# The norms of the second block beside its last products, on one Trainium2 core

## The reference

```
x = layer_norm(ALPHA * x + gate * out, g, b)        # out: mixer or mlp, gate: one row of 1024 per stream
z = x * (1 + scale) + shift                          # the next product's input
```

## Time and profile before

| What | Value |
|---|---|
| time, median of 3 runs | 2361.1 us (2357.43 to 2363.76) |
| the profiled execution's own time | 2361.36 us |
| its span | 2359.6 us |
| TensorE matmul busy | 2093.7 us (89%) |
| VectorE busy | 1306.8 us (55%) |
| ScalarE busy | 866.1 us (37%) |
| GpSimd busy | 229.3 us (10%) |
| mean granted clock of TensorE | 0.937 |

### The profile page before, as it was taken

The page is one execution under the profiler, slowest core; times in us unless marked ns, Lnnn a source line. Parts: engine busy times, 40 slices in busy tenths (PEclk is TensorE's granted clock), DMA queues, the critical chain, the costliest instruction groups (busy, mean ns, idle before and its releaser), DMA issues.

```text
span 2359.6 us, 31254 instructions
## 1 busy us (share of the span) xinstructions
PE 2093.7 (89%) x12126; PEld 1734.4 (74%) x12126; DVE 1306.8 (55%) x2032; ACT 866.1 (37%) x1435; POOL 229.3 (10%) x233
## 2 busy tenths in 40 slices
PE   6978899979788999599999993999999398996995
PEld 5856699878567998477777773888888387775985
DVE  4464677574646774454544448444444724756665
ACT  4422266344222663323223223322322323643442
POOL 1010200000101000000000004000000520612002
PEclk8999899989998999799999995999999699997998
DMA  7466556544664655222122231233323143433661
GB/s 204 135 230 203 168 166 181 188 125 135 226 215 138 178 178 196 83 72 89 53 89 71 71 89 36 90 92 93 100 89 104 35 111 108 60 77 110 191 188 54
DMA packets 304172, 296.26 MB, mean 126 GB/s; under 512 B 10390, under 2 KB 223586, under 8 KB 303952
## 3 DMA queue, kind: packets, MB, share of 16 engines
q1 hardware_dynamic: 297184, 276.86, 38.5%
q0 software_dynamic: 6896, 18.13, 3.6%
HBM read 293.90 MB, written 1.05 MB: 125 GB/s over the span
## 4 chain that ended last, share of the span: by engine, by line
PE 79%; DVE 14%; ACT 3%; issue 2%; DMA 1%; POOL 1%; SPq 0%; DVEq 0%; ACTq 0%; POOLq 0%
PE ps L422 22%; PE ps L423 22%; PE ps L424 22%; DVE w_lo L411 2%; PE ps L2048 2%; PE ps L1689 2%; PE ps L488 2%; DVE small L1367 1%; DVE zt_lo L1522 1%; PE ps L665 1%; PE ps L2038 1%; DVE hid L1422 1%; PE ps L663 1%; PE ps L1537 1%; DVE y L1573 1%
## 5 line engine op out<-in xcount | busy, mean ns | idle before, releaser
L411 DVE TENSOR_TENSOR w_lo<-raw,w_hi 128x1024 fp32r<-128x1024 f32 x428 | 505.7, 1223 | 439.5 <-ACT w_hi L403 439.2
L403 ACT ACTIVATE w_hi<-raw 128x1024 fp32r<-128x1024 f32 x428 | 428.9, 1051 | 667.1 <-PE ps L422 534.9
L422 PE MATMUL ps<-zt_hi,w_hi 128*128 128x512 f32 (+1 forms) x768 | 270.2, 352 | 21.0 <-DVE zt_lo L1522 12.2
L422 PE MATMUL ps<-xt_hi,w_hi 128*128 128x256 f32 x896 | 260.4, 291 | 21.9 <-DVE xt_lo L1100 10.7
L423 PE MATMUL ps<-zt_lo,w_hi 128*128 128x512 f32 (+1 forms) x768 | 269.0, 350 | 0.0
L424 PE MATMUL ps<-zt_hi,w_lo 128*128 128x512 f32 (+1 forms) x768 | 268.9, 350 | 0.0
L423 PE MATMUL ps<-xt_lo,w_hi 128*128 128x256 f32 x896 | 255.2, 285 | 0.0
L424 PE MATMUL ps<-xt_hi,w_lo 128*128 128x256 f32 x896 | 255.0, 285 | 0.0
L422 PEld LDWEIGHTS ps<-xt_hi,w_hi 128*128 128x128 f32 x896 | 173.1, 193 | 29.7 <-issue 12.8
L422 PEld LDWEIGHTS ps<-zt_hi,w_hi 128*128 128x128 f32 x768 | 146.4, 191 | 43.3 <-DVE zt_lo L1522 12.9
L423 PEld LDWEIGHTS ps<-xt_lo,w_hi 128*128 128x128 f32 x896 | 173.2, 193 | 0.0
(11 more groups left out here) (358 smaller groups left out, 3591.9 us busy)
## 6 DMA issues: line engine op xcount, KB each, us to landing
raw<-in_mlp_w SPq DMA_DIRECT2D x128, 512.0 KB, 4.6
raw<-in_ada_w SPq DMA_DIRECT2D x96, 512.0 KB, 5.0
raw<-in_w_up SPq DMA_DIRECT2D x88, 512.0 KB, 5.0
raw<-in_w_in SPq DMA_DIRECT2D x56, 512.0 KB, 4.7
raw<-in_ret_w_in SPq DMA_DIRECT2D x48, 512.0 KB, 4.4
raw<-in_w_down SPq DMA_DIRECT2D x44, 512.0 KB, 4.0
raw<-in_nat_w_in SPq DMA_DIRECT2D x24, 512.0 KB, 4.7
raw<-in_w_out SPq DMA_DIRECT2D x16, 512.0 KB, 5.3
```

Source lines behind the costliest of these rows:

```text
L403: nc.scalar.activation(w_hi[:, t, w], raw[:, s, w], ACT.Copy).then_inc(on("w_hi"), act.gives("w_hi"))
L411: ins = nc.vector.tensor_tensor(w_lo[:, t, w], raw[:, s, w], w_hi[:, t, w].bitcast(F32), ALU.subtract)
L422: first = nc.tensor.matmul(out_ap, l_hi, r_hi, start=start, stop=False)
```

## The change

The norms' work is the same, its place is another. The parts:
- gate_b gets a place of its own (nat's nd now shares it; rtmp moves onto rt_lo). The gates for the retention are spread before the first block's last norm, those for the nat behind its second query-key unit. No diagonals any more: the stationary operand is the gate column itself, broadcast, and the moving one the identity.
- the last two down units (retention's last head, taken out of the loop, and the first mlp's last) run in pairs of token tiles (`pe_down_norm4`), with the transposes among the products; all 8 PSUM banks are used. VectorE runs the halves of each tile as they come (`dve_norm4`, `dve_half`); gate times y and ALPHA times x for what is known before are done earlier (`dve_ahead`).
- GpSimd's residual stream (`pool_stream`) starts only when the last tile's low part is written; GpSimd's gains are loaded after the powers.
- the next stage starts by tile (`rows_by_tile`, nat) or by stream (`up_by_stream`, mlp); in the nat's output product the second unit of each half ends tile by tile.
- the clearing of y stands behind the first up step. At the end g and b are folded into two VectorE operations of 1024 per tile (`dve_final`), and each tile is stored by its own DMA.

```diff
@@ placement in SBUF @@
+        gate_b = s2("gate_b", [2, D])
-        gate_b = sm("gate_b", [2, D])
+        nd = gate_b[:, 1, :].rearrange("p (b h q) -> p b h q", b=2, h=4)
...
+        def pe_gates(pe, l, chunk, streams):
+            for s in streams:
                 for k in range(KT):
-                    ins = T.matmul(ps[4 + 2 * s + k // 4][:, hs(k % 4)], ones, xf2[:, s, k, :], start=True, stop=True)
+                    ins = T.matmul(ps[4 + 2 * s + k // 4][:, hs(k % 4)],
+                                   mod[:, l, 8 * chunk + k, s:s + 1].to_broadcast([P, P]), ident, start=True, stop=True)
                 ins.then_inc(on("gate_ps"), pe.gives("gate_ps"))
...
+        def dve_ahead(dve, c, tiles):
+            for t in tiles:
+                V.tensor_tensor(y[:, t, half(c)], y[:, t, half(c)], gate_b[:, stream_of(t), half(c)], ALU.mult).then_inc(
+                    on("v_step"), dve.gives("v_step"))
+            dve.eng.wait_ge(on("v_step"), dve.given("v_step"))
+            for t in tiles:
+                V.scalar_tensor_tensor(x_of(t)[:, half(c)], x_of(t)[:, half(c)], ALPHA, y[:, t, half(c)],
+                                       ALU.mult, ALU.add).then_inc(on("v_step"), dve.gives("v_step"))
+        def dve_half(dve, c, t, bank, form):
+            x, yt, gate = x_of(t)[:, half(c)], y[:, t, half(c)], gate_b[:, stream_of(t), half(c)]
+            if form != "fresh":
+                dve.eng.wait_ge(on("dn_ps"), dve.takes("dn_ps"))
+            if form == "added":
+                V.tensor_tensor(yt, yt, ps[bank][:, :], ALU.add).then_inc(on("y_add"), dve.gives("y_add"))
+                dve.eng.wait_ge(on("y_add"), dve.given("y_add"))
+                V.tensor_tensor(yt, yt, gate, ALU.mult).then_inc(on("v_step"), dve.gives("v_step"))
+                dve.eng.wait_ge(on("v_step"), dve.given("v_step"))
+            else:
+                sem = "v_step" if form == "fresh" else "y_add"
+                V.tensor_tensor(yt, ps[bank][:, :], gate, ALU.mult).then_inc(on(sem), dve.gives(sem))
+                dve.eng.wait_ge(on(sem), dve.given(sem))
+            if form == "ahead":
+                V.tensor_tensor(x, x, yt, ALU.add).then_inc(on("v_step"), dve.gives("v_step"))
+            else:
+                V.scalar_tensor_tensor(x, x, ALPHA, yt, ALU.mult, ALU.add).then_inc(
+                    on("v_step"), dve.gives("v_step"))
+            dve.eng.wait_ge(on("v_step"), dve.given("v_step"))
+            o = 32 * (t % 2) + 6 * c
+            V.bn_stats(small[:, o:o + 6], x).then_inc(on("v_step"), dve.gives("v_step"))
+            if c == 1:
+                o = 32 * (t % 2)
+                dve.eng.wait_ge(on("v_step"), dve.given("v_step"))
+                V.bn_aggr(small[:, o + 12:o + 14], small[:, o:o + 12]).then_inc(on("v_step"), dve.gives("v_step"))
+                dve.eng.wait_ge(on("v_step"), dve.given("v_step"))
+                V.tensor_scalar(small[:, o + 16:o + 17], small[:, o + 13:o + 14], LN_EPS, None, ALU.add).then_inc(
+                    on("pow_in"), dve.gives("pow_in"))
+        def dve_normal(dve, t):
+            dve.eng.wait_ge(on("pow_out"), dve.takes("pow_out"))
+            o = 32 * (t % 2)
+            V.tensor_scalar(y[:, t, :], x_of(t), small[:, o + 12:o + 13], small[:, o + 16:o + 17],
+                            ALU.subtract, ALU.mult).then_inc(on("zn"), dve.gives("zn"))
...
+        def pe_down_norm4(pe, h_hi_, h_lo_, ready=None, y_banks=False):
+            hi, lo = {}, {}
+            def product(c, t, unit_ends=False):
+                if c == 0 and ready:
+                    pe.eng.wait_ge(on(ready), pe.takes(ready))
+                if c == 1 and y_banks:
+                    pe.eng.wait_ge(on("y_add"), pe.beyond("y_add", t + 1))
+                x = slice(t * P, (t + 1) * P)
+                for k in range(4):
+                    w = slice(512 * k, 512 * k + 512)
+                    first, last = three(ps[4 * c + t][:, :], h_hi_[:, k, x], h_lo_[:, k, x], hi[c][:, w], lo[c][:, w],
+                                        k == 0, k == 3)
+                    if k == 0 and unit_ends:
+                        begun(pe, first)
+                last.then_inc(on("dn_ps"), pe.gives("dn_ps"))
+            def turned(t, ends_unit=False):
                 pe.eng.wait_ge(on("zn"), pe.takes("zn"))
+                pe_turned(pe, y[:, t, :], (t, 4 + t), ends_unit)
+            hi[0], lo[0] = unit_slot(pe)
+            product(0, 0, True)
+            product(0, 1)
+            hi[1], lo[1] = unit_slot(pe)
+            product(1, 0)
+            product(1, 1)
+            product(0, 2)
+            product(0, 3)
+            turned(0)
+            product(1, 2, True)
+            turned(1)
+            product(1, 3)
+            turned(2, True)
+            turned(3)
+            pe.used["y_add"] += 8
+        def act_norm4(act, coefs):
+            for t in ALL:
+                act_turned(act, t, (t, 4 + t), coefs[stream_of(t)])
+                if t in (0, 3):
+                    split_hi(act)
+        def dve_norm4(dve, form):
+            open_hh(dve)
+            dve_half(dve, 0, 0, 0, form[0])
+            dve_half(dve, 0, 1, 1, form[0])
+            dve_half(dve, 1, 0, 4, form[1])
+            dve_half(dve, 1, 1, 5, form[1])
+            dve_normal(dve, 0)
+            dve_half(dve, 0, 2, 2, form[0])
+            dve_normal(dve, 1)
+            dve_half(dve, 0, 3, 3, form[0])
+            split_lo(dve)
+            dve_half(dve, 1, 2, 6, form[1])
+            dve_turned(dve, 0)
+            dve_normal(dve, 2)
+            dve_half(dve, 1, 3, 7, form[1])
+            dve_turned(dve, 1)
+            dve_normal(dve, 3)
+            dve_turned(dve, 2)
+            dve_turned(dve, 3)
+            split_lo(dve)
...
+        def pool_gains2(pool, l, m):
             pool.eng.wait_ge(on("zs_new"), pool.given("zs_new"))
             for j, v in enumerate(("ln_g_2", "ln_b_2")):
                 pool.eng.dma_start(gn2[:, j, :], a[v][l, m].partition_broadcast(P)).then_inc(
                     on("gn2_in"), pool.gives("gn2_in", 16))
...
+        def pool_stream(pool, tiles):
+            pool.eng.wait_ge(on("gn2_in"), pool.takes("gn2_in", 32))
+            pool.eng.wait_ge(on("zT"), pool.takes("zT", len(tiles)))
+            for t in tiles:
...
@@ pe_ret, the last of the four heads, out of the loop @@
+            if last_head:
+                pe_down_norm4(pe, rt_hi, rt_lo, ready="rt")
+            else:
...
@@ dve_head, after the scores @@
+            if last_head:
+                dve.eng.wait_ge(on("y_add"), dve.given("y_add"))
+                dve.eng.wait_ge(on("gate_b"), dve.takes("gate_b", 4))
+                for c in range(2):
+                    dve_ahead(dve, c, ALL)
...
@@ pe_mlp @@
+            def up_by_stream():
+                pe.eng.wait_ge(on("hh"), pe.takes("hh", 2))
+                hi, lo = unit_slot(pe)
+                for n in range(2):
+                    x = slice(n * SEQ, (n + 1) * SEQ)
+                    pe.eng.wait_ge(on("zT"), pe.takes("zT", NT))
+                    for f in range(2):
+                        for k in range(KT):
+                            c = f * 1024 + k * P
+                            first, last = three(ps[f][:, x], hi[:, c:c + P], lo[:, c:c + P], zt_hi[:, k, x],
+                                                zt_lo[:, k, x], k == 0, k == KT - 1)
+                            if n == f == k == 0:
+                                begun(pe, first)
+                last.then_inc(on("up_ps"), pe.gives("up_ps"))
             def step(what, b, c):
+                if len(tiles) == 4 and c is last_down:
+                    pe.eng.wait_ge(on("hh"), pe.takes("hh", 4))
+                    pe_down_norm4(pe, hh_hi[:, b, :, :], hh_lo[:, b, :, :], y_banks=True)
+                    return
...
@@ dve_mlp @@
+                        if j == 0 and dve.loop is None:
+                            dve.eng.wait_ge(on("y_add"), dve.given("y_add"))
+                            dve.eng.wait_ge(on("gate_b"), dve.takes("gate_b", 2 * len(streams)))
+                            dve_ahead(dve, 0, tiles)
+                if what == "up" and dve.loop is None and c == 0:
+                    dve.eng.wait_ge(on("zs_new"), dve.takes("zs_new", len(tiles)))
+                    for t in tiles:
+                        V.memset(y[:, t, :], 0.0).then_inc(on("y_zero"), dve.gives("y_zero"))
+                    dve.eng.wait_ge(on("y_zero"), dve.given("y_zero"))
...
+        def dve_final(dve):
+            dve_half(dve, 0, 2, 4, "ahead")
+            dve_half(dve, 0, 3, 5, "ahead")
+            dve_half(dve, 1, 2, 6, "added")
+            dve_half(dve, 1, 3, 7, "added")
+            dve.eng.wait_ge(on("gn2_in"), dve.takes("gn2_in", 128))
+            for t in LAT:
+                dve.eng.wait_ge(on("pow_out"), dve.takes("pow_out"))
+                o = 32 * (t % 2)
+                V.scalar_tensor_tensor(y[:, t, :], x_of(t), small[:, o + 12:o + 13], gn2[:, 0, :],
```

(44 more changed lines are left out.)

524 lines of the change are left out of this document (246 added, 278 removed).

## The result

The changed kernel takes 2269.9 us in the median of 4 runs (2266.83 to 2272.38), beside 2362.4 us for the kernel before in 4 runs of the same chip: a ratio of 0.9611 (95% interval 0.9591 to 0.9631). The forecast was 2271 us. The profiled execution took 2268.4 us with a span of 2266.6.

What follows compares the result with a forecast made beforehand. VectorE's chain bounds four places, TensorE the rest. Savings 39.8 + 28.1 + 13.1 + 10.8, less 0.5 and 1.5, give 89.8 us: 2271 from a median of 2361.1; own range 2263 to 2280, 8 in 10 2258 to 2288.

Steps and rivals of the forecast that it cites:

- A and B: Norms after the retention and after the first mlp: next stage starts sooner, saving 39.8 and 28.1 us.
- C0: Time zero for schedules in A and B: the first matmul of the last two down units.
- C: Norm after the neighbourhood attention: the mlp starts at 2139.8 instead of 2152.92, saving 13.1 us.
- The 1.95 us of gates: Attention's projections, where TensorE bounds: the 16 gate matmuls moved there add 1.95 us.
- D: Kernel's end: half 0 hides and the store starts at 2344.4 instead of 2355.19, saving 10.8 us.
- the 4.4 us that I left as they were: Kernel's end: time from the store's start to the span's end, taken as unchanged; at best 2 us shorter.
- The stream's contention: GpSimd's residual stream under the next stage's first units slows VectorE's splits: 0.5 us, kept 0 to 9.
- one of the prediction's own signs of being wrong: First three units after A or B: TensorE waiting for w_lo or hh_lo would show the forecast wrong.
- The clearing: Last mlp's first down unit: y's memsets behind the first up step cost 1.5 us of wait (0 to 2.1).
- Contention through two GpSimd operations: Rival: a VectorE operation beside the stream is held through two GpSimd operations, some 13 us: 2284; chance 0.12.
- The start by tile: In A and B the next stage starts before the last tile is through; rival: it doesn't, 2281, chance 0.11.
- The straight-line last head: Rival: the unrolled last head's code, fetched as it runs, slows some 430 matmuls; 2387 at 0.5 us each; chance 0.02.

Runs made afterwards that it cites:

- e6: Kernel before, with only the gates spread early and placed as in the changed kernel: 2351.5 us, ratio 0.9956.
- e9: Changed kernel, but the last two down units run in unit order, all turns behind all products, instead of pairs of tiles: 2268.7 us, ratio 0.9608.
- e5: Changed kernel, but VectorE's split of the next stage's first unit stands behind the last tile's normal: 2258.8 us, ratio 0.9557.
- e4_nostream: Changed kernel, but GpSimd's two residual-stream operations touch one column instead of 1024: 2269.8 us, ratio 0.9603.
- e1_whole: Changed kernel, but the next stage waits for all four turned tiles after the retention and after the first mlp: 2280.8 us, ratio 0.9654.
- e7: Changed kernel, but one 1 MB store behind both tiles' last operation instead of two of 512 KB: 2272.1 us, ratio 0.9612.
- b1: Changed kernel with the late split, and GpSimd's stream in pieces of 256 columns with a wait ahead of every operation: 2258.2 us, ratio 0.9556.
- e2: Changed kernel, but GpSimd's multiply and add run right behind each tile's normal, as before the change: 2284.2 us, ratio 0.9676.
- e10: Changed kernel, but y is not cleared ahead of the last mlp: 2267.9 us, ratio 0.9594.
- e3: Changed kernel, but GpSimd's stream goes in pieces of 256 columns, four multiplies then four adds per tile: 2270.6 us, ratio 0.96.

## Why the prediction was right, step by step

- **A and B** (39.8 and 28.1 forecast, 40.1 and 29.5 measured). The chain ran as scheduled: next starts at C0 + 35.7 and 37.4 against 36.0 and 38.8, the split standing at C0 + 22.9 and 23.1 for 3.46 and 2.47 us (forecast 22.0 and 2.5), turns of tiles 2 and 3 at 1.97. e6 confirms the share of the gates in A, 9.1 us. That their 32 matmuls cost nothing ahead of the first block's last norm is so: before, TensorE stood 8.58 us there for the first turn, and now it does the gates in 3.82 us and then stands 5.00. e9 shows that the step "in pairs" wasn't needed, and e5 that the order which I scheduled wasn't the best: 3.9 and 4.3 us lay in that standing split.
- **C** (13.1). 16.1 us behind the last product were forecast and 16.2 measured. The 1.95 us of gates are seen in the trace at their new place (16 matmuls, 1.95), but the stretch between B and C did not grow. Windows of 20 us around TensorE's two waits ahead of the attention's scores show why, in the kernel before, the changed kernel and e4_nostream (the last figures are granted clock, DMA share, GB/s):

```profile
1990.00:2010.00 20.00, 13.30 (x83) 8.40 (x84) 12.38 (x36) 12.34 (x30) 6.68 (x10) 0.74 0.32 46
...
1924.00:1944.00 20.00, 13.24 (x91) 8.55 (x90) 13.01 (x37) 12.95 (x32) 7.03 (x11) 0.83 0.34 50
...
1929.00:1949.00 20.00, 13.22 (x75) 7.98 (x74) 11.77 (x34) 11.53 (x28) 5.54 (x9) 0.74 0.39 63
```

The granted clock was 0.74 before and 0.83 in the changed kernel's trace, worth 0.09 x 20 = 1.8 us (my estimate). With 0.74 again, e4_nostream, whose code from B to C has the gates too, takes 247.0 us in place of 245.2; with 0.83, e1_whole takes 245.1. So the 1.95 us are there, and the clock in this one trace hid them: luck, not a step of mine. What decides the clock there no run shows. e6 gives 5.4 us of C to the gates.
- **D** (10.8, measured 12.5). The mis-sized term is the 4.4 us that I left as they were: e7 shows that storing tile by tile is worth 1.4 us, within the "at best 2 us" that I named and didn't take. The other 0.4 is a chain 0.45 us shorter (last VectorE operation at 8.85 us behind the last matmul, 9.3 forecast). The last section of the prediction says 20 us between the last matmul and the end: a slip against its own sum, which gives 13.7; measured are 11.9.
- **The stream's contention** (0.5, measured 2.45 as a wait). The first split beside the stream took 6.71 us in A and 6.72 in B, where I had 6.6, and the others 4.5 to 6.5. TensorE never waited for a second or third unit's low part, in A or in B. The margin that broke was one that I had named and then let pass: the low part of the hidden units in A, 63.5 against 64.0. It ended at C0 + 65.1, because the two of them took 5.63 us, and TensorE had wanted it at 62.8. So one of the prediction's own signs of being wrong, a wait for hh_lo in the first three units after A, did come. e4 takes that wait away with the stream, and b1 with shorter holds. The prediction also says that an operation with one tensor in SBUF is not held; the normal reads one and was (e2), which cost nothing here, because no normal lies beside the stream in the changed kernel.
- **The clearing** (1.5, measured 1.49 as a wait); e10 shows the cause. The 1.07 us that the prediction gives to one is the time from one start to the next; the row it names has 0.91 for one operation.
- **The rivals.** Contention through two GpSimd operations did not occur in the changed kernel (3.4 us per operation), and e3 shows that it isn't impossible: there one was held through some seventeen short ones. The start by tile is real (e1). The straight-line last head ran as the loop had: from the third head's last product to C0 it took 86.7 us, against 87.4 before.

That the forecast came within 1.1 us of the median (2271 against 2269.9) owes something to luck. The errors have both signs: D, B and the stretch between B and C came out 1.7, 1.4 and 1.95 us better than forecast, the contention 1.9 worse. And the kernel before took 2362.4 us in these runs, where the forecast started from 2361.1; the saving is 92.5 us against 89.8.

## What to carry to other kernels

Schedule the chain behind a stage's last products engine by engine, in us from their first matmul, and look first for an instruction that stands for another engine ahead of work that is ready: one moved line was worth 9 us by the traces and 11 by the medians, as much as the gates. Pieces of a norm beside the products brought the gain in both orders of the products that were tried. When work is moved under the next stage, check every value that the stage wants in that time, the smallest margin first, and not only the weights.

## What the runs showed of the hardware

- Beside GpSimd's stream, a VectorE operation with two SBUF tensors waits for whole GpSimd instructions, and its turn does not always come with the next one. With 1024-element GpSimd operations a VectorE operation stood for one of them (splits of 6.7 us); with pieces of 256 and a wait after each, or after every second, for one piece (splits of 2.9 to 3.5); with four multiplies and four adds back to back one VectorE operation of 1.2 us stood for 13.6 us, to the end of the stream. Both long splits began while adds ran, but so did one of 3.34 in C; in the splits that began among multiplies each operation was held through one piece at most (2.89 to 3.39). Which condition decides stays open.
- A normal (subtract and multiply with two columns as scalars, one tensor read) was held like an operation with two tensors, 2.83 us against 0.80 in e2_early, while the statistics of the same run kept their 0.69 inside a GpSimd operation of the stream (at 1413.30). The Trainium skill lists this in "SBUF — State Buffer", section "Who interferes with whom": tensor_scalar can take the shared ports in its fast modes. The trace agrees.
- A turn of 8 matmuls took 1.97 us behind 2.44 and 5.67 us of idle TensorE in A (granted clock 0.50 in the turn, the 1.2 GHz level), and 1.09 behind 0.96 us in e5_late (granted 1.00, the 2.4 GHz level): the shorter wait also made the turn shorter.
